# Differential heads with token-major value products, row sums on ACT and two transposes back, in place of a sum by ones over 256 columns

## The reference, cut to what matters

```
probs = softmax(causal(q k^T * scale - slopes * dist))     # (B, H, 2, Q, K)
a = probs[:, :, 0] - lam * probs[:, :, 1]
o = einsum('bhqk,bkhe->bqhe', a, v)                        # per head: 256 tokens x 128
o = rms_norm(o, g_diff_sub) * (1 - 0.2)                    # norm over the 128 columns
y_diff = o.reshape(256, 1024) @ w_branch_diff
```

## Time and profile of the kernel before

| | us |
|---|---|
| median of 3 runs | 908.86 |
| lowest and highest | 908.78, 909.88 |
| the profiled execution | 907.51 |
| its span in the trace | 906.3 |
| PE busy | 898.1 (99%) |
| DVE busy | 681.8 (75%) |
| ACT busy | 477.2 (53%) |
| POOL busy | 66.3 (7%) |

### The profile page before, as it was taken

How to read it: one execution, slowest core, us unless ns; L and a number is a source line. 1 busy time by engine, 2 the same in 40 slices (tenths; PEclk the granted TensorE clock), 3 DMA queues, 4 the chain that set the end, 5 groups by cost and what they waited for, 6 DMA issues and landing times.

```text
span 906.3 us, 17826 instructions
## 1 busy us (share of the span) xinstructions
PE 898.1 (99%) x7186; PEld 869.0 (96%) x7186; DVE 681.8 (75%) x1210; ACT 477.2 (53%) x844; POOL 66.3 (7%) x136
## 2 busy tenths in 40 slices
PE   9999999999999999999999999999999999999997
PEld 7899999999999999998999989999999999999997
DVE  7776676778988788889789877786767666666677
ACT  5366355555655545566466644554345544444466
POOL 7023100120000000000001000000102000000001
PEclk9999999999999999999999999999999999999999
DMA  8553443645565655655644363666646666666651
GB/s 314 166 158 120 144 132 118 188 148 164 163 196 178 188 182 188 187 185 170 199 144 125 110 209 115 187 187 184 186 141 192 204 187 186 187 187 186 187 150 60
DMA packets 42257, 154.16 MB, mean 170 GB/s; under 512 B 4672, under 2 KB 5184, under 8 KB 42048
## 3 DMA queue, kind: packets, MB, share of 16 engines
q1 hardware_dynamic: 42176, 153.03, 54.6%
HBM read 151.96 MB, written 1.05 MB: 169 GB/s over the span
## 4 chain that ended last, share of the span: by engine, by line
PE 98%; DVE 1%; DMA 0%; issue 0%; ACT 0%; SPq 0%; DVEq 0%
PE bank L279 97%; DMA xc<-in_xT 0%; PE bank L837 0%; PE bank L460 0%; DVE va L1986 0%; DVE work L1505 0%; DVE wl L1340 0%; PE bank L675 0%; PE bank L463 0%; PE bank L676 0%; PE bank L462 0%; PE bank L677 0%; PE bank L464 0%; PE bank L461 0%; DVE a1l L1344 0%
## 5 line engine op out<-in xcount | busy, mean ns | idle before, releaser
L1340 DVE TENSOR_TENSOR wl<-raw,wh 128x1024 fp32r<-128x1024 f32 x282 | 349.0, 1246 | 94.1 <-ACT wh L880 92.3
L880 ACT ACTIVATE wh<-raw 128x1024 fp32r<-128x1024 f32 x247 | 258.3, 1053 | 152.4 <-PE bank L279 143.0
L279 PE MATMUL bank<-a2h,wh 128*128 128x256 f32 x896 | 253.6, 284 | 0.0
L279 PE MATMUL bank<-a2h,wl 128*128 128x256 f32 x896 | 250.3, 280 | 0.0
L279 PE MATMUL bank<-a2l,wh 128*128 128x256 f32 x896 | 248.3, 280 | 0.0
L279 PE MATMUL bank<-a1h,wh 128*128 128x258 f32 (+1 forms) x800 | 226.1, 284 | 0.7 <-issue 0.6
L279 PE MATMUL bank<-a1h,wl 128*128 128x258 f32 (+1 forms) x800 | 223.7, 281 | 0.0
L279 PE MATMUL bank<-a1l,wh 128*128 128x258 f32 (+1 forms) x800 | 220.2, 282 | 0.0
L279 PEld LDWEIGHTS bank<-a2h,wh 128*128 128x128 f32 x896 | 168.7, 188 | 3.0 <-issue 2.7
L279 PEld LDWEIGHTS bank<-a2h,wl 128*128 128x128 f32 x896 | 168.5, 188 | 0.0
L279 PEld LDWEIGHTS bank<-a2l,wh 128*128 128x128 f32 x896 | 167.5, 188 | 0.3
(11 more groups left out here) (258 smaller groups left out, 1024.4 us busy)
## 6 DMA issues: line engine op xcount, KB each, us to landing
raw<-in_wts SPq DMA_DIRECT2D x284, 512.0 KB, 3.7
csb<-in_cst SPq DMA_DIRECT2D x1, 1364.0 KB, 9.3
out<-va SPq DMA_DIRECT2D x2, 512.0 KB, 3.0
xc<-in_xT SPq DMA_DIRECT2D x1, 816.0 KB, 7.0
xc<-in_xT SPq DMA_DIRECT2D x1, 276.0 KB, 4.2
va<-in_pT SPq DMA_DIRECT2D x1, 256.0 KB, 3.9
ccol<-in_fcst SPq DMA_DIRECT2D x1, 154.0 KB, 6.4
gr<-in_lamv SPq DMA_DIRECT2D x1, 128.0 KB, 9.1
```

Of the source, the lines that this page charges most:

```text
L279: return e.matmul(o, lhsT, rhs, start=start, stop=stop, skip_group_check=True)
L880: e.activation(wh[:, i % NHL, :], raw[:, i % NRAW, :], ACT.Copy).then_inc(s_hi, 1)
L1340: e.tensor_tensor(lo, src, hi.bitcast(F32), ALU.subtract).then_inc(s_lo, 1)
```

## The change

It moves the value product to token-major: the transposed probabilities become the stationary operand, in three 128-column products (queries 0 to 127, and queries 128 to 255 against two blocks of keys), so that tokens lie on the partitions. The sum of squares of a token is then a row sum, which ACT accumulates while it squares (two instructions of 128 columns with `accum_out`, in place of one of 256). The clamps, logarithms, addition and root work on 128 x 2 numbers in a new small buffer `dsm`. `diff_scale` is one small instruction and two `tensor_scalar` of 128 columns. Then two PE transposes (`diff_back`) bring the head back to feature-major, in columns 256 to 511 of its bank; `diff_hi` reads them there, with the gain as its scale, and `diff_lo` reads the bank too.

In the list of slots: the sum at V+4 goes. Parts move from V+5 to V+3, logs and the POOL addition from V+6 to V+4, root from V+7 to V+5, scale from V+8 to V+6; `diff_back` stands at V+8 and waits for scale; hi moves from V+9 to V+8 and lo from V+10 to V+9. The value product of head h (h of 2 and above) now waits for `s_ya`, which is `diff_lo(h-2)`, because lo is now the last reader of the bank.

```diff
@@ tensor_engine
                 if h < 2:
                     e.wait_ge(s_va, 12)
                 else:
-                    e.wait_ge(s_dr, 2 * (h - 2) + 1)
-                mm(o[:, 0:S], vh(0), at[:, 0:256], True, False)
-                mm(o[:, 128:S], vh(1), at[:, 256:384], False, True).then_inc(s_do, 1)
-
-            def diff_sum(h):
+                    e.wait_ge(s_ya, h - 1)
+                mm(o[:, 0:128], at[:, 0:128], vh(0), True, True)
+                mm(o[:, 128:S], at[:, 128:256], vh(0), True, False)
+                mm(o[:, 128:S], at[:, 256:384], vh(1), False, True).then_inc(s_do, 1)
+
+            def diff_back(h):
                 o = bank[B_O2[h % 2]]
-                e.wait_ge(s_dsq, h + 1)
-                mm(o[:, S:2 * S], ones, qk[:, 8 + h, 0:S], False, True).then_inc(s_dss, 1)
+                e.wait_ge(s_dr, 3 * h + 3)
+                e.transpose(o[:, S:S + 128], qk[:, h, 0:128], ident)
+                e.transpose(o[:, S + 128:2 * S], qk[:, h, 128:S], ident).then_inc(s_dbk, 1)
...
-                    elif j == DIFF_AV[h] + 4:
-                        diff_sum(h)
+                    elif j == DIFF_AV[h] + 8:
+                        diff_back(h)
@@ scalar_engine
             def diff_square(h):
                 e.wait_ge(s_dx, h + 1)
-                e.activation(qk[:, 8 + h, 0:S], qk[:, h, 0:S], ACT.Square, scale=2.0 ** -10).then_inc(s_dsq, 1)
+                for b in range(2):
+                    c = slice(b * 128, b * 128 + 128)
+                    e.activation(qk[:, 8 + h, c], qk[:, h, c], ACT.Square, scale=2.0 ** -10,
+                                 accum_out=d_ss(h)[:, b:b + 1]).then_inc(s_dsq, 1)
...
             def diff_hi(h):
-                e.wait_ge(s_dr, 2 * h + 2)
-                e.activation(a1h[:, h, 0:S], qk[:, h, 0:S], ACT.Copy).then_inc(s_dh, 1)
+                e.wait_ge(s_dbk, h + 1)
+                e.wait_ge(s_lmd, 5)
+                e.activation(a1h[:, h, 0:S], bank[B_O2[h % 2]][:, S:2 * S], ACT.Identity, scale=small[:, 53:54]).then_inc(s_dh, 1)
...
-                    elif a == 6:
+                    elif a == 4:
                         diff_logs(h)
-                    elif a == 7:
+                    elif a == 5:
                         diff_root(h)
-                    elif a == 9:
+                    elif a == 8:
                         diff_hi(h)
@@ vector_engine
             def diff_scale(h):
-                x, v2 = qk[:, h, 0:S], qk[:, 8 + h, 0:S]
-                ss = bank[B_O2[h % 2]][:, S:2 * S]
                 e.wait_ge(s_dw, h + 1)
-                e.scalar_tensor_tensor(v2, ss, BIG, v2, ALU.is_lt, ALU.mult).then_inc(s_dr, 1)
-                e.wait_ge(s_dr, 2 * h + 1)
-                e.wait_ge(s_lmd, 5)
-                e.scalar_tensor_tensor(x, x, gdiff, v2, ALU.mult, ALU.mult).then_inc(s_dr, 1)
+                e.scalar_tensor_tensor(d_v2(h), d_ss(h), BIG, d_v2(h), ALU.is_lt, ALU.mult).then_inc(s_dr, 1)
+                e.wait_ge(s_dr, 3 * h + 1)
+                for b in range(2):
+                    x = qk[:, h, b * 128:b * 128 + 128]
+                    e.tensor_scalar(x, x, d_v2(h)[:, b:b + 1], None, ALU.mult).then_inc(s_dr, 1)
 
             def diff_lo(h):
                 e.wait_ge(s_dh, h + 1)
-                low(a1l[:, h, 0:S], qk[:, h, 0:S], a1h[:, h, 0:S]).then_inc(s_ya, 1)
+                e.scalar_tensor_tensor(a1l[:, h, 0:S], bank[B_O2[h % 2]][:, S:2 * S], gdiff, a1h[:, h, 0:S].bitcast(F32),
+                                       ALU.mult, ALU.subtract).then_inc(s_ya, 1)
...
-                    elif a == 5:
+                    elif a == 3:
                         diff_parts(h)
-                    elif a == 8:
+                    elif a == 6:
                         diff_scale(h)
-                    elif a == 10:
+                    elif a == 9:
                         diff_lo(h)
```

More of the change, by code:

```diff
@@ L154, in program @@
         onesb = sb("onesb", [P, 128])
+        dsm = sb("dsm", [P, 8, 6])
         cfh = a2h[0:104, :, :].rearrange("p a b -> p (a b)")[:, 0:L]
@@ L221, in program @@
         s_ds, s_db, s_dm, s_de, s_dn, s_dt, s_dc = (sem(f"s_{n}") for n in ("ds", "db", "dm", "de", "dn", "dt", "dc"))
-        s_do, s_dx, s_dsq, s_dss, s_dv, s_dl = (sem(f"s_{n}") for n in ("do", "dx", "dsq", "dss", "dv", "dl"))
+        s_do, s_dx, s_dsq, s_dbk, s_dv, s_dl = (sem(f"s_{n}") for n in ("do", "dx", "dsq", "dbk", "dv", "dl"))
         s_dp, s_dr, s_dw, s_dh, s_ya = (sem(f"s_{n}") for n in ("dp", "dr", "dw", "dh", "ya"))
@@ L262, in program @@
         PLE_BANK = (5, 6, 1, 2)
+        d_ss = lambda h: dsm[:, h, 0:2]
+        d_v1 = lambda h: dsm[:, h, 2:4]
+        d_v2 = lambda h: dsm[:, h, 4:6]
         r_ret = lambda h: work[:, 4 * (h % 2) + 1, 0:S]
@@ L711, in ret_av @@
                     e.wait_ge(*ev2(27))
-                    e.wait_ge(s_dr, 2 * (6 + par) + 1)
+                    e.wait_ge(s_ya, 7 + par)
                 else:
@@ L1158, in diff_square @@
                 e.wait_ge(s_dx, h + 1)
-                e.activation(qk[:, 8 + h, 0:S], qk[:, h, 0:S], ACT.Square, scale=2.0 ** -10).then_inc(s_dsq, 1)
+                for b in range(2):
+                    c = slice(b * 128, b * 128 + 128)
+                    e.activation(qk[:, 8 + h, c], qk[:, h, c], ACT.Square, scale=2.0 ** -10,
+                                 accum_out=d_ss(h)[:, b:b + 1]).then_inc(s_dsq, 1)
             def diff_logs(h):
-                v1, v2 = tmpb[:, h % 6, 0:S], qk[:, 8 + h, 0:S]
                 e.wait_ge(s_dv, 2 * h + 1)
-                e.activation(v1, v1, ACT.Ln, bias=eps, scale=2.0 ** 13).then_inc(s_dl, 1)
+                e.activation(d_v1(h), d_v1(h), ACT.Ln, bias=eps, scale=2.0 ** 13).then_inc(s_dl, 1)
                 e.wait_ge(s_dv, 2 * h + 2)
-                e.activation(v2, v2, ACT.Ln, scale=2.0 ** -50).then_inc(s_dl, 1)
+                e.activation(d_v2(h), d_v2(h), ACT.Ln, scale=2.0 ** -50).then_inc(s_dl, 1)
             def diff_root(h):
-                v2 = qk[:, 8 + h, 0:S]
                 e.wait_ge(s_dp, h + 1)
-                e.activation(v2, v2, ACT.Exp, scale=-0.5).then_inc(s_dw, 1)
+                e.activation(d_v2(h), d_v2(h), ACT.Exp, scale=-0.5).then_inc(s_dw, 1)
             def diff_hi(h):
-                e.wait_ge(s_dr, 2 * h + 2)
-                e.activation(a1h[:, h, 0:S], qk[:, h, 0:S], ACT.Copy).then_inc(s_dh, 1)
+                e.wait_ge(s_dbk, h + 1)
+                e.wait_ge(s_lmd, 5)
+                e.activation(a1h[:, h, 0:S], bank[B_O2[h % 2]][:, S:2 * S], ACT.Identity, scale=small[:, 53:54]).then_inc(s_dh, 1)
             def ret_square(h):
@@ L1770, in diff_parts @@
             def diff_parts(h):
[L1771 to L1776 removed]
+                e.wait_ge(s_dsq, 2 * h + 2)
+                e.tensor_scalar(d_v1(h), d_ss(h), 2.0 ** 50, None, ALU.min).then_inc(s_dv, 1)
+                e.tensor_scalar(d_v2(h), d_ss(h), 2.0 ** 50, BIG, ALU.max, ALU.min).then_inc(s_dv, 1)
             def diff_scale(h):
[L1779 to L1780 removed]
                 e.wait_ge(s_dw, h + 1)
[L1782 to L1785 removed]
+                e.scalar_tensor_tensor(d_v2(h), d_ss(h), BIG, d_v2(h), ALU.is_lt, ALU.mult).then_inc(s_dr, 1)
[3 more added lines that the diff above has]
+                    e.tensor_scalar(x, x, d_v2(h)[:, b:b + 1], None, ALU.mult).then_inc(s_dr, 1)
             def diff_lo(h):
                 e.wait_ge(s_dh, h + 1)
[L1789 removed]
+                e.scalar_tensor_tensor(a1l[:, h, 0:S], bank[B_O2[h % 2]][:, S:2 * S], gdiff, a1h[:, h, 0:S].bitcast(F32),
+                                       ALU.mult, ALU.subtract).then_inc(s_ya, 1)
             def ret_decay(h):
@@ L2060, in gpsimd_engine @@
                 for h in range(8):
-                    if p == DIFF_AT[h] + DIFF_AV[h] + 6:
-                        v2 = qk[:, 8 + h, 0:S]
+                    if p == DIFF_AT[h] + DIFF_AV[h] + 4:
                         e.wait_ge(s_dl, 2 * h + 2)
-                        e.tensor_tensor(v2, tmpb[:, h % 6, 0:S], v2, ALU.add).then_inc(s_dp, 1)
+                        e.tensor_tensor(d_v2(h), d_v1(h), d_v2(h), ALU.add).then_inc(s_dp, 1)
             mix_add(16, S)
```

6 lines of the change are left out of this document (removed).

## The result

| | before | changed |
|---|---|---|
| runs, median (us) | 908.82 (908.56 to 909.88, 4 runs) | 918.38 (917.86 to 919.25, 4 runs) |
| ratio to before, 95% interval | | 1.0105 [1.0092, 1.0117] |
| profiled execution (us) | 907.51 | 918.05 |
| its span (us) | 906.3 | 916.8 |

The changed kernel is 1.05% slower. The forecast was 917.1 us in a range of 913.5 to 920.0, with 0.92 for slower.

A forecast was written before the change was run, and what follows sets the result against it. PE was taken to bound the kernel (busy 99%, 98% of the last chain). Waits of 9.8 us less 1.6 us of PE's work gave +8.2: profiled execution 915.7, median 917.1 us, range 913.5 to 920.

The forecast's parts named there:

- The bound: PE is busy 99% and 98% of the last chain: work saved is won in full, new waits lost in full.
- PE's own work: Eight heads on PE: two transposes replacing the sum by ones win 1.7 us, value products cost 0.1; net -1.6 us.
- the handover: From DVE's low part to PE's value product, with a weight load that can't run ahead: 0.1 us.
- The waits: Value products of heads 2 to 7 wait on PE for the low part of two heads earlier: 9.8 us.
- ACT's chain (heads 3, 5, 7): Transposes to low part, through ACT's block copy, outlast PE's 3.07 us: waits 1.3 us at heads 3 and 5, 0.5 at 7.
- DVE's backlog (heads 2, 4, 6): DVE's queued work delays the low part: waits of 1.9 us at heads 2 and 4, 2.9 at 6; together 6.7.
- The rule on narrow instructions: On DVE and ACT, fixed cost per instruction: by columns alone ACT chains some 0.4 us shorter, whole change some 1 us better.
- Hidden: Rival: DVE finishes the low part before PE ends the tile, so only PE's work counts: 907.3 us; chance 0.06.
- Only DVE's backlog: Rival: heads 3, 5 and 7 wait about nothing, leaving +6.7 - 1.6: 914.0 us; chance 0.14.
- Narrow as dear as wide: Rival: narrow parts, scale, square and logs on DVE and ACT cost as much as wide, +2.0: 919.1 us; chance 0.12.
- The clock falls: Rival: after waits up to 2.9 us PE could drop to 1.2 GHz, six tiles costing 17 us: 934; chance 0.03.
- The sum: Whole kernel: waits 9.8 and PE -1.6 give +8.2; profiled execution 907.51 becomes 915.7, median 917.1 us.

The follow-up runs named there:

- e1_no_lo_wait: Changed kernel with the low part read from SBUF instead of the bank (wrong values), so value products wait only for the high part; 907.59 us, 0.9994.
- e7_square_later: Changed kernel with the squares of heads 2 and 4 one slot later on ACT; 916.75 us, 1.0081 of before.
- a0_after_again: Changed kernel, unaltered, profiled in one more execution; 918.49 us.
- e4_all_but_head4: Changed kernel with transposes, high and low part one slot earlier for all heads but head 4; 911.82 us, 1.0040 of before.
- e6_again: Second profiled execution of the kernel before with only the new wait added (value product waits for the low part of two heads earlier); 924.64 us.
- e6_before_plus_wait: Kernel before with only the new wait added: value product waits for the low part of two heads earlier instead of that head's scale; 922.93 us, 1.0157.
- e9_scale5_first: Changed kernel with transposes, high and low part one slot earlier, and head 5's scale on DVE ahead of tile 20's cast; 907.21 us, 0.9976 of before.
- e0_before: Kernel before, unchanged, timed against itself for a second trace; 909.21 us, 1.0002.
- e5_lo_before_block: Changed kernel with DVE's low part ahead of the weight block's low part, for head 4 also ahead of tile 20's cast; 910.26 us, 1.0010 of before.
- e9_again: Repeat with more rounds: changed kernel with transposes, high and low part earlier and head 5's scale ahead of tile 20's cast; 906.81 us, 0.9975 of before.

## Why the prediction was right

**The bound.** PE is the chain, nothing later gives a loss back: right, shown by the sums of the stretches, where the waits that were taken away came back in full. The one exception is small: head 6's wait, taken away alone, returned 2.3 of its 2.75 us, since head 7's grew.

**PE's own work.** Forecast -1.6, measured -1.7 by e1_no_lo_wait. The six products of an unstalled value product start over 0.67 us (0.66 forecast), two transposes over 0.22 before the next tile's first matmul. One term was left out: the restart of a waiting value product, 0.08 us each, 0.5 in all. The prediction had only the handover in its chains.

**The waits.** By head, start to start:

| head | 2 | 3 | 4 | 5 | 6 | 7 | sum |
|---|---|---|---|---|---|---|---|
| forecast (us) | 1.9 | 1.3 | 1.9 | 1.3 | 2.9 | 0.5 | 9.8 |
| measured (us) | 1.85 | 1.16 | 1.85 | 1.15 | 2.91 | 0.57 | 9.5 |

*ACT's chain (heads 3, 5, 7).* Head 3 in the rows of the changed kernel, first ACT, then DVE; the transposes start at 482.00:

```profile
482.42 0.48 ACT L1183 ACTIVATE a1h<-bank,small 128x256 fp32r<-128x256 f32 x1 [3.22 <-PE bank L700]
482.80 0.30 ACT L1167 ACTIVATE qk<-qk 128x128 f32<-128x128 f32 x1
483.00 0.19 ACT L1167 ACTIVATION_READ_ACCUMULATOR qk<-qk 128x1 f32 x1
483.09 0.30 ACT L1167 ACTIVATE qk<-qk 128x128 f32<-128x128 f32 x1
...
483.38 1.05 ACT L886 ACTIVATE wh<-raw 128x1024 fp32r<-128x1024 f32 x1
```
```profile
484.46 1.22 DVE L1348 TENSOR_TENSOR wl<-raw,wh 128x1024 fp32r<-128x1024 f32 x1 [0.52 <-ACT wh L886]
485.61 0.48 DVE L1793 SCALAR_TENSOR_TENSOR a1l<-bank,small,a1h 128x256 fp32r<-128x256 f32 x1
```

Every link of the forecast is there, in its order: 0.42 until ACT sees the transposes (0.42 forecast), high part 0.38 (0.41), square 0.58 (0.77), block copy 1.08 (1.05), `lo_to` 1.15 (1.17), low part and handover 486.23 - 485.61 = 0.62 (0.56). Together 4.23 against 4.38, less PE's 3.07: 1.16. The mis-sized term is the square: its row was read from a 128-column exponential of 0.39 us, and a square of that width from SBUF takes 0.30, 0.20 to its accumulator read. e7_square_later took those 0.58 us out and the wait shrank by just so much. Head 7, without a square, has 0.57 by the same links.

*DVE's backlog (heads 2, 4, 6).* Head 2 in DVE's timeline, from the scale of head 0 on. Left out are the rest of the four maxima and their reads (1.30 us from first start to the next block, as forecast), an eviction at 472.66 and the rest of the combine behind its first instruction at 473.41:

```profile
469.15 0.42 DVE L1887 TENSOR_TENSOR qk<-bank,rb 128x256 f32<-128x256 f32 x1 [0.71 <-PE bank L283]
469.49 0.15 DVE L1785 SCALAR_TENSOR_TENSOR dsm<-dsm 128x2 f32<-128x2 f32 x1
469.68 0.48 DVE L1789 TENSOR_SCALAR qk<-qk,dsm 128x128 f32<-128x128 f32 x2
470.08 0.28 DVE L1752 CUSTOM_DVE_ANT_0 work<-bank,work 128x128 f32<-128x128 f32 x1
...
471.38 1.22 DVE L1348 TENSOR_TENSOR wl<-raw,wh 128x1024 fp32r<-128x1024 f32 x1
472.52 0.16 DVE L1780 TENSOR_SCALAR dsm<-dsm 128x2 f32<-128x2 f32 x1
472.59 0.16 DVE L1781 TENSOR_SCALAR dsm<-dsm 128x2 f32<-128x2 f32 x1
...
473.41 0.18 DVE L1762 RECIPROCAL smallh<-smallh 128x4 f32<-128x4 f32 x1 [0.33 <-ACT work L1154]
...
475.26 1.22 DVE L1348 TENSOR_TENSOR wl<-raw,wh 128x1024 fp32r<-128x1024 f32 x1
476.40 0.48 DVE L1793 SCALAR_TENSOR_TENSOR a1l<-bank,small,a1h 128x256 fp32r<-128x256 f32 x1
```

Combine takes 475.26 - 473.41 = 1.85 (1.85 forecast), `lo_to` 1.14 (1.13), low part to PE's start 0.62 (0.56). The scale is 0.59 instead of 0.72 and the parts 0.14 instead of 0.2; that reading was too dear, and the low part's end a little too cheap. At head 6 the combine begins only at 517.27, after DVE has stood for 1.79 us waiting for the exponentials of head 7; then come eviction, cast (0.72), block (1.14) and the low part, in the order that the prediction named, for 2.91 against 2.9. "Backlog" is thus too loose a word: DVE is not busy all the way, the exponentials on ACT are a link of these three chains.

**The rule on narrow instructions.** The two clamps of `diff_parts` on 128 x 2 numbers last 0.16 us each on DVE, where a `tensor_scalar` of 128 columns lasts 0.29 (L1769, at 473.88 us). On ACT a square of 128 columns takes 0.30 us, and a logarithm of 2 columns 0.19 to 0.28. A width 64 times as small saves about half of an instruction's own time, or less. That agrees with the Trainium skill, "VectorE: DVE Perf Modes", section "The TRN2 errata", on a fixed cost per instruction. But what a chain pays is the distance to the next start, and there narrow is cheaper: 0.07 us between the two clamps, 0.20 for each `tensor_scalar` of 128 columns in the scale (469.68 to 470.08 for two). And the four instructions of the square pair overlap so well that the pair costs 0.58 us: between the 0.4 by columns alone and the 0.77 taken.

**The rivals.** *Hidden* (907.3): refuted by six waits. The same change a slot earlier has 907.34, but that it is the same number is chance: it was measured beside a kernel before of 908.06, and its stretch is 0.8 us shorter than before, not 1.6. *Only DVE's backlog* (914.0): refuted by 1.16, 1.15 and 0.57 us at heads 3, 5 and 7. *Narrow as dear as wide* (919.1): refuted, the error was on the other side. *The clock falls* (934, chance 0.03): this one happened, and was thought of wrongly in chance and in size. The argument against it was that PE is busy for 5 us between waits. That work ahead of the wait did not keep the clock up behind the 2.75 us wait in any of the four profiles that have it (changed, a0_after_again, e4_all_but_head4, e7_square_later). And six falls of a whole tile were priced, where one came, of 1.5 us. The other argument, that no row of the trace before shows a fall, missed its end: PE's last matmul ends at 901.34 us, and in the stretch from 903 to 904 us the granted clock is 0.84, from 904 on 0.50, so it fell 2.3 us after PE had stopped. With a wait of 2.9 us in the forecast, that was a reason for a higher chance than 0.03. The Trainium skill, "TensorE: Matmul & The Clock Gate", section "What's actually happening", says that an idle array falls back to half rate; the rows above agree, and they put it at standstills of about 2.5 us and more.

**The sum.** Forecast 915.7 for the profiled execution: -1.6 + 9.8. Measured 918.05, of which the heads account for -1.7 + 9.5 + 0.5 (restarts) + 1.5 (clock) = 9.8 against the 8.2 forecast. The other 0.7 us lies outside the heads' stretch; 0.65 of it is in the 55 us behind the heads, which the last section comes to. So the execution came out 2.3 us above its forecast: 1.6 in the heads (2.0 for the two terms that were missing, less 0.3 and 0.1 for waits and products taken too dear) and 0.7 outside. The median, 1.3 us above the forecast, is within the range. That it missed by 1.3 and not by 2.3 is luck: the profiled execution lay 1.35 us below the median in the kernel before, which the forecast carried over, but only 0.3 below it in the changed one.

## What to carry to other kernels

Before a buffer's last reader changes, find out where the new last reader stands in its engine's order and what is queued ahead of it: here one wait moved from an early reader to a late one cost 11.5 us with what it did to the clock, though three engines had less to do, and one slot of difference took all but 0.9 us of it away. Count such a wait as a chain of starts on every engine from the point that both sides share, and compare it with PE's own way to the same place. And if a new wait comes near 2.5 us, add a fall of the clock: here it came in six of ten waits of 2.48 to 2.88 us, and cost 1.3 to 2.6 us.

## What the runs showed that was not expected

The clock: six of ten standstills of 2.48 to 2.88 us were followed by 3 to 7 us at 1.2 GHz, which by the heads' stretches cost 1.3 to 1.5 us in the five cases of 3 to 4 us and 2.6 in the one of nearly 7 (e6_again: 107.77 - 92.79 - 11.0 - 6 x 0.24, rounded). None followed the shorter ones (1.70 us or less). The same program had its fall at different places in two executions, so a single profile does not tell which wait is to blame.

The matmuls' pitch: in the 55 us behind the heads (565 to 620 us in the kernel before) the same 128 x 256 products start 117.3 ns apart in the profile of before, 118.7 in that of the changed kernel, and 120.0 in e6_before_plus_wait and e9_scale5_first, with a granted clock of 1.00 each time. That looked like a second cost of the change. It is none: the kernel before in another execution (e0_before) has 118.7, e5_lo_before_block 117.3 and e9_again 118.7. Over 55 us the three levels are 0.6 us apart. It happens in a second stretch too, ahead of the heads and so ahead of everything that the change touches: from 250 to 400 us eleven profiles have 117.2 ns and three (e0_before, e6_again, e7_square_later) 118.5 to 118.6, which is 1.0 of the 1.6 us by which e0_before reaches the heads later than before. Elsewhere all profiles agree more closely (118.1 to 118.7 in the heads, 118.2 behind 620 us). What sets the levels was not tried.

> The kernel before once more, unchanged, for a second trace. Between 565 and 620 us its first trace has PE start matmuls every 117.3 ns, and the changed kernel and all its variants so far 118.7 ns, which makes 0.6 us. Theory P (something in the change makes that stretch slower): 117.3 ns again. Rival Q (that trace was a quick one of the kernel before, as its 907.51 us against a median of 908.1 to 908.9 suggest): 118.7 ns here too, and a time equal to the kernel before within 0.1%.

Measured: 909.21 us, 1.0002 [0.9992, 1.0011]. The kernel compared with itself gives the size of what such a comparison can tell, 0.1%.

Left open: e1_no_lo_wait and the two runs of e9_scale5_first have the same heads' stretch to 0.05 us, but 0.9994 and 0.9976 of before. The first interval reaches down to 1.4 us less, the others up to 1.4 us less, so they only just meet, beside the 1.7 us of the stretch. Most of the difference lies in the kernel before, whose median was 908.06 us beside e1_no_lo_wait and 909.10 and 909.31 beside the other two; the variants' own medians lie within 0.8 us (907.59, 907.21, 906.81). Whether the chips make this, or the levels of the pitch above, was not settled.
